# Latent attention: logits and maximum in one VectorE instruction; selected attention: meta products on 128 rows

## The reference, cut to what matters

```python
def dsa_attention(q, k, v, iq, ik, iw, rel_bias, chunk, valid, topk):   # 8 heads of 64
    ...
        _, idx = lax.top_k(score, topk)
        kg = take(k, idx)
        vg = take(v, idx)
        logits = jnp.einsum('bqhd,bqkhd->bhqk', qb, kg).astype(jnp.float32) * dh ** -0.5
        bias = rel_bias[rel_bucket(idx - qpos[None, :, None])]
        logits = logits + jnp.transpose(bias, (0, 3, 1, 2)).astype(jnp.float32)
        logits = jnp.where(ok[:, None], logits, NEG_INF)
        p = jax.nn.softmax(logits, axis=-1).astype(v.dtype)
        return jnp.einsum('bhqk,bqkhd->bqhd', p, vg)
```

```python
def causal_attention(q, k, v):
    ...
        sc = jnp.einsum('bqhd,bkhd->bhqk', qb, k,
                        preferred_element_type=jnp.float32) * scale
        qpos = start + jnp.arange(Q_BLOCK)
        sc = jnp.where(kpos[None, :] <= qpos[:, None], sc, -jnp.inf)
        p = jax.nn.softmax(sc, axis=-1)
        return jnp.einsum('bhqk,bkhd->bqhd', p.astype(v.dtype), v)
```

## Time and profile before

| what | value |
|---|---|
| three timed runs | 2734.92, 2715.95 and 2737.76 us (median 2734.92) |
| the profiled execution | 2732.96 us |
| its span, from its first to its last instruction | 2731.2 us |
| mean granted TensorE clock in it | 0.975 of full speed |
| TensorE busy | 2621.8 us |
| VectorE, ScalarE, GpSimd busy | 1047.4, 881.9 and 1075.9 us |

### The profile page before, as it was taken

How to read it: one execution, slowest core, us unless ns; L and a number is a source line. 1 busy time by engine, 2 the same in 40 slices (tenths; PEclk the granted TensorE clock), 3 DMA queues, 4 the chain that set the end, 5 groups by cost and what they waited for, 6 DMA issues and landing times.

```text
span 2731.2 us, 32116 instructions
## 1 busy us (share of the span) xinstructions
PE 2621.8 (96%) x13277; PEld 2146.3 (79%) x13277; DVE 1047.4 (38%) x1740; ACT 881.9 (32%) x1289; POOL 1075.9 (39%) x830
## 2 busy tenths in 40 slices
PE   7999899999998999999889999999999999999999
PEld 6888787887566888877677888878888788888887
DVE  3656343424447322255555222252121444421212
ACT  4433322324654222233534222242222322322221
POOL 3223122431114444444205444445444445444443
PEclk9999987998999999999999999999999999999999
DMA  4222000321013233231103233232233232233222
GB/s 127 63 63 84 27 16 16 109 78 47 16 47 103 94 95 105 89 91 49 55 9 108 94 94 106 85 100 93 93 101 99 88 98 93 93 98 100 96 93 77
DMA packets 215852, 217.78 MB, mean 80 GB/s; under 512 B 10600, under 2 KB 213091, under 8 KB 215707
## 3 DMA queue, kind: packets, MB, share of 16 engines
q1 hardware_dynamic: 215504, 215.68, 24.7%
q10 hardware_dynamic: 202, 0.06, 0.0%
HBM read 213.60 MB, written 2.12 MB: 79 GB/s over the span
## 4 chain that ended last, share of the span: by engine, by line
PE 88%; DVE 5%; ACT 3%; issue 2%; POOL 1%; DMA 1%; ACTq 0%; DVEq 0%; SPq 0%
PE ps L490 65%; PE ps L486 8%; PE ps L493 4%; PE ps L804 2%; PE ps L773 2%; POOL wl L466 1%; ACT wh L459 1%; PE ps L788 1%; PE ps L2417 1%; PE ps L2028 1%; PE ps L1992 1%; PE ps L1475 0%; PE ps L1972 0%; DMA raw<-in_w_in_ab 0%; DVE rstd L567 0%
## 5 line engine op out<-in xcount | busy, mean ns | idle before, releaser
L466 POOL TENSOR_TENSOR wl<-raw,wh 128x512 fp32r<-128x512 f32 x794 | 1047.3, 1350 | 1541.9 <-ACT wh L459 1541.9
L490 PE MATMUL ps<-NH,wh 128*128 128x512 f32 (+1 forms) x1824 | 721.0, 395 | 22.0 <-POOL wl L466 11.3
L490 PE MATMUL ps<-NL,wh 128*128 128x512 f32 (+1 forms) x1824 | 715.8, 392 | 0.0
L490 PE MATMUL ps<-NH,wl 128*128 128x512 f32 (+1 forms) x1824 | 715.0, 392 | 0.0
L459 ACT ACTIVATE wh<-raw 128x2048 fp32r<-128x2048 f32 (+4 forms) x219 | 380.6, 1738 | 479.8 <-PE ps L490 429.3
L490 PEld LDWEIGHTS ps<-NH,wh 128*128 128x128 f32 (+1 forms) x1824 | 345.1, 189 | 104.5 <-POOL wl L466 14.4
L490 PEld LDWEIGHTS ps<-NL,wh 128*128 128x128 f32 (+1 forms) x1824 | 344.7, 189 | 74.8 <-issue 1.7
L490 PEld LDWEIGHTS ps<-NH,wl 128*128 128x128 f32 (+1 forms) x1824 | 344.8, 189 | 73.5
L490 PE MATMUL ps<-GH,wl 128*128 128x512 f32 x832 | 332.8, 400 | 0.0
L490 PE MATMUL ps<-GH,wh 128*128 128x512 f32 x832 | 329.8, 396 | 2.3 <-DVE GL L728 2.3
L490 PE MATMUL ps<-GL,wh 128*128 128x512 f32 x832 | 329.6, 396 | 0.0
(11 more groups left out here) (390 smaller groups left out, 3099.9 us busy)
## 6 DMA issues: line engine op xcount, KB each, us to landing
raw<-in_ffn_w_gate SPq DMA_DIRECT2D x44, 1024.0 KB, 5.4
raw<-in_ffn_w_up SPq DMA_DIRECT2D x44, 1024.0 KB, 5.3
raw<-in_ffn_w_down SPq DMA_DIRECT2D x32, 1024.0 KB, 4.9
raw<-in_w_in_ab SPq DMA_DIRECT2D x16, 1024.0 KB, 5.5
raw<-in_w_in_cd SPq DMA_DIRECT2D x14, 1024.0 KB, 5.0
raw<-in_ffn_w_down SPq DMA_DIRECT2D x16, 768.0 KB, 4.2
raw<-in_c_w_in SPq DMA_DIRECT2D x12, 1024.0 KB, 5.1
raw<-in_w_out_ab SPq DMA_DIRECT2D x8, 512.0 KB, 3.4
```

Of the source, the lines that this page charges most:

```text
L466: ins = nc.gpsimd.tensor_tensor(wl[:, b % 2, ks, 0:w], raw[:, b % 2, ks, 0:w], wh[:, b % 2, ks, 0:w].bitcast(F32), ALU.subtract)
L490: last = nc.tensor.matmul(ps[0:m1 - m0, bank, 0:SEQ], w[:, s, k, m0:m1], x(k), start=start, stop=stop)
```

## The change

Latent attention gets a flag `negated`. With it VectorE's logits are one `tensor_tensor_reduce`: scores plus bias, times the negated root, and the minimum over the row goes to `mmx`. The separate maximum is gone. The buffer `mlg` then holds the negated logits and `mmx` the negated maximum, as before; ScalarE's exponential takes them with scale -1 instead of 1 and waits for the semaphore of the logits. The negated root is made once for all heads and tiles, by a VectorE instruction between the two reciprocals.

In selected attention the meta product of the values uses all 128 partitions of `pt` and of tile 0 of `av`. So that the rows beyond 16 add nothing, VectorE fills tile 0 of `av` with zero ahead of the top-k rounds, and the columns 512 to 639 of both buffers of `pt` ahead of the attention loop. ScalarE's first eviction of `av` waits for the first fill (`av_zero`). This also goes for the meta query tile, in which the products have 16 output rows. The tables of dense and unread products are the same.

```diff
@@ soft_pe, values(i)
             kts = ([0] if A.meta else []) + list(range(1, t + 1))
             for x, kt in enumerate(kts):
-                kn = META if kt == 0 else P
                 a0 = 4 * P if kt == 0 else (kt - 1) * P
-                last = nc.tensor.matmul(ps[0:n, A.value_at[i % len(A.value_at)], 256:256 + HD], A.pt[0:kn, i % 2, a0:a0 + n], A.v(kt, h),
+                last = nc.tensor.matmul(ps[0:n, A.value_at[i % len(A.value_at)], 256:256 + HD], A.pt[:, i % 2, a0:a0 + n], A.v(kt, h),
                                         start=(x == 0), stop=(x == len(kts) - 1))
@@ soft_dve, logits(i)
             s0 = A.score_at[i % len(A.score_at)]
+            if A.negated:
+                nc.vector.tensor_tensor_reduce(out=A.lg[0:n, i % 2, 0:w], in0=ps[0:n, s0, 0:w], in1=b, scale=A.scale(t, n, h), scalar=BIG,
+                                               op0=ALU.add, op1=ALU.min, accum_out=A.mx[0:n, i % 2, :]).then_inc(S(tg + "_logits"), 1)
+                return
@@ soft_act, exps(i)
-            act.wait_ge(S(tg + "_max"), i + 1)
+            act.wait_ge(S(tg + ("_logits" if A.negated else "_max")), i + 1)
...
-            nc.scalar.activation(A.lg[0:n, i % 2, 0:w], A.lg[0:n, i % 2, 0:w], ACT.Exp, bias=A.mx[0:n, i % 2, :],
+            nc.scalar.activation(A.lg[0:n, i % 2, 0:w], A.lg[0:n, i % 2, 0:w], ACT.Exp, bias=A.mx[0:n, i % 2, :], scale=-1.0 if A.negated else 1.0,
@@ the object mla
-               None, mla_between, one_bank=True)
+               None, mla_between, one_bank=True, negated=True)
@@ second_dve
         step(dve, nc.vector.reciprocal(qroot[:, :, :], qroot[:, :, :]))
+        step(dve, nc.vector.tensor_scalar(qroot[:, :, :], qroot[:, :, :], -1.0, None, ALU.mult))
@@ the object dsa
-               lambda kt, h: av[0:token_tile(kt)[1], kt, h * HD:(h + 1) * HD],
+               lambda kt, h: av[:, kt, h * HD:(h + 1) * HD],
@@ ScalarE, the evictions of av
+            if name == "av" and i == 0:
+                act.wait_ge(S("av_zero"), 1)
@@ VectorE's list
         index_dve(dve)
+        nc.vector.memset(av[:, 0, :], 0.0).then_inc(S("av_zero"), 1)
         for _ in topk_steps(dve, (0, 1)):
...
+        step(dve, nc.vector.memset(pt[:, :, 4 * P:5 * P], 0.0))
         soft_dve(dve, dsa, lambda e: e.wait_ge(S("strip_out"), HEADS))
```

More of the change, by code:

```diff
@@ L27 @@
 NEG = -1e30
+BIG = 3e38
 TAKEN = -3e38
@@ L740, in __init__ @@
         def __init__(self, tag, tiles, q, k, v, width, scale, bias, off, lg, pt, oa, mx, gate, tile0, meta, banks, fill=None, between=None,
-                     oa_first=None, gate_ready=None, spare=None, one_bank=False):
+                     oa_first=None, gate_ready=None, spare=None, one_bank=False, negated=False):
             self.tag, self.tiles, self.q, self.k, self.v = tag, tiles, q, k, v
@@ L747, in __init__ @@
             self.oa_first, self.gate_ready, self.spare, self.one_bank = oa_first, gate_ready, spare, one_bank
+            self.negated = negated
             self.own_mix = self.mix_at not in self.score_at and self.mix_at != self.meta_at
```

## The result

The changed kernel takes 2700.25 us (median of 12 runs, 2693.87 to 2705.71); the kernel before, run beside it, 2714.86 us (12 runs, 2710.85 to 2737.76). The ratio of the means is 0.9932, with a 95% interval of 0.9908 to 0.9956: faster by 0.7%, less than the forecast 1%. The forecast time of 2707 us is 7 us too long, and the forecast gain, 28 us, is twice the 14.6 us between the medians.

A forecast was written before the change was run, and what follows sets the result against it. TensorE, busy 2621.8 of 2731.2 us, was taken as the bound, through its waits, product spacing and clock. 2733 - 5 (rows) - 18 (clock) - 3.5 (fused) + 0.3 (small instructions) gave 2707 us; range 2699 to 2727 us.

The forecast's parts named there:

- within 1%: Whole kernel: time about the same as before, chance 0.50, against faster 0.46 and slower 0.04.
- clock term: Selected attention: the 47.8 us stretch at the lower clock goes or is short; 18 us taken.
- worked-out 22.6 us: Selected attention: 47.8 us at the lower clock become 25.2 us at the full clock with its waits.
- row edit: Selected attention, meta products on all rows: 0.29 us a step; 5 us taken, between 0 and 9.3.
- count of 18 steps: Selected attention: 32 steps less 6 waiting for H and 8 with gate work gain, 5.2 us.
- Rival 2: Selected attention: the row edit changes neither spacing nor clock; 2730 us, chance 0.05.
- fused instruction: Latent attention: logits and maximum in one shrink 12 TensorE waits by 0.33 us each; 3.5 us taken.
- Rival 3: Latent attention: the fused instruction is slow and VectorE becomes the bound; 2763 us at 3.5 us each, chance 0.04.
- small steps: Negated root +0.2 us on the path; fills of av and pt 0, av up to 0.5; +0.3 in the sum.
- Rival 1: Selected attention: the low clock stays, since the wait preceding it is not removed; 2725 us, chance 0.15.

The follow-up runs named there:

- spare_24_25: Kernel before with six unread products also ahead of the scores of steps 24 and 25, 16 rows kept; median 2714.66 us.
- rows_not_t3: Changed kernel with the 16 rows back in the third query tile alone (steps 24 to 31); median 2702.92 us.
- fused_only: Kernel before with only the fused instruction in latent attention, meta products still on 16 rows; median 2711.21 us.
- rows_only: Changed kernel without the fused instruction: only the 128 rows of the meta products and the two fills; median 2703.64 us.
- rows_not_22_24: Kernel before with meta products on 128 rows in all steps but 22, 23 and 24, no fused instruction; median 2708.08 us.

## Why the prediction was right or wrong

The sign, the range of 2699 to 2727 us and "within 1%" as the likeliest of the three were right; the size of the gain was not. Without the clock term the forecast was 8.2 us, and 11.2 were measured.

*The step that failed is the clock term*, "The runs price it lower ... I take 18 us": it was taken off 2733 us in full, as if every execution of the kernel before had the long fall. The mechanism was right. The lower level is gone in every execution, the row edit alone does it, and where it occurs it costs 20.7 us in tiles 2 and 3 (49.28 against 30.6 us in `spare_24_25` and `rows_not_t3`, and 30.48, of which 4 us are at the lower clock, against 28.5) and 25.8 us between the medians of the two kinds, so even the worked-out 22.6 us was nearer than the 18 that was taken. Where the other 5 of the 25.8 us lie was not found. The greater error is what the term was subtracted from. Three runs had two of the upper kind, and the prediction let their median stand for the kernel; 42 of 105 have it, and in the 12 runs of the comparison 3 had. The median beside which the change was measured, 2714.86 us, is of the lower kind, and has nothing of this term in it. The mean has: 11.2 us between the lower kinds and 3 of 12 times 25.8 us make 17.7 us, and the means are 18.4 us apart (2718.7 and 2700.3). The run at 2715.95 us was read rightly as the kernel without the fall, but it lies 4.5 us above the median of its kind, which makes up most of what 18 us were short. That the forecast time was nevertheless only 6.6 us off is no support for its parts: from the profiled execution to the lower kind of before are 21.6 us instead of 18, and from there to the changed kernel 11.2 instead of 8.2. The stage from the first step of tile 1 to the last of tile 4 is 27.8 us shorter (134.4 and 106.6), 20.7 by the clock and the rest by the rows; "22 us or so" were forecast. The forecast should have been a median for each kind.

*The row edit*: forecast 5 us, between 0 and 9.3; measured 7.8. The gap is gone wherever it was. The count of 18 steps was too low: the 6 waits for H and the 8 steps with gate work were taken to give nothing, but the waits for H and for the exponential grew by 1.3 and 1.8 us only. Why by so little was not tested; VectorE's scaling waits for the values too, and moves up with them. Rival 2 is refuted, and with it the use that was made there of the rule on LDWEIGHTS in the Trainium skill.

*The fused instruction*: forecast 3.5 us, measured 4.8 by `fused_only`, 3.4 by the changed kernel against `rows_only`, and 5.0 in the stage without the short stretch. The main instruction was priced exactly. What was wrong is "VectorE is shorter by 486 - 154 = 332 ns a step": the readback is 82 ns and not 154, and lengths were subtracted where the start times give 0.51 us, since the readback runs beside the next instruction and the old maximum waited for the end of the logits. Twelve waits times 0.51 us would be 6.1 us; that 5.0 came fits the forecast's remark that shorter waits end at zero. Of the two reasons given, the scaling behind VectorE's load counts for more than the place of the maximum in the chain. Rival 3, the slow instruction, did not come.

*The small steps*: the negated root takes 182 ns as forecast from the nearest row, and the two fills are hidden.

*Rival 1*: it rested on the wait for H ahead of the fall, which indeed stays. It does not decide the clock.

*Sums that do not come out*: with the bounds as given, the forecast's own range begins at 2697 us and not at 2699, rival 1 goes from 2715 to 2736 and not from 2717 to 2732, and with the low clock kept an excess of 1.5 us, not 1.6, makes rival 3 slower. No reading of the result hangs on these.

## What to carry to other kernels

When the same kernel's runs fall into two heaps, find what parts them and forecast each heap; a median of three is a toss-up between them. In this kernel a product on 64 rows or fewer among products on more cost 0.2 to 0.3 us for the way in and out, so padding with zeros to 96 or 128 rows can be worth a fill. If the clock falls at one place, try the two or three steps there first. A fused reduction pays mostly by the time it takes off its engine: read that time from start to start, and follow it to the next instruction that waits for that engine.

## What the runs showed of the hardware that was not expected

- Products on 16 and on 64 rows among products on 128 have the same price, 0.27 us a step with way in and out (0.33 us by the start times of one step, before the waits behind it grow); on 96 rows there is none.
- VectorE's readback of its accumulator takes 82 ns, half of a 128x1 reciprocal (154 ns), and the next instruction starts in the same moment (1370.10 us in the changed kernel); the fused add, scale and minimum is as fast as the plain scale and add (751 and 750 ns at 512).
- TensorE's clock fell in two microseconds in which it was busy for 1.51 and 1.48 us, and stayed in full in two others with the same 1.51 and 1.48. Once there, the lower level lasted for 44.4 us (`rows_not_22_24`) and 47.8 us (before), in which TensorE never paused. The Trainium skill, TensorE: Matmul & The Clock Gate, section Part 1: The HAM clock gate, ties the lower level to how busy the engine has been; the busy times of these rows do not part the two cases.
